# Output weights prepared inside the last unit of a layer, and the last attention begun behind the first half tile: a two-layer hybrid decoder step

## The reference

```python
u = rms_norm(x, norm_gain)
proj = einsum('btd,dc->btc', u, w_in)            # 1024 -> 3592 columns
h_m = sigmoid(mo) * mlstm(mq, mk, mv, gates)     # 4 heads, chunked memory
h_r = retention(rope(rq), rope(rk), rv)          # 4 heads, chunked memory
h_a = window_attention(aq, ak, av, sinks, bias)  # 8 heads, window 128
mix = concat(head_norm(h_m) * silu(mz), head_norm(h_r) * silu(rz), h_a * silu(az))
x = x + einsum('btc,cd->btd', mix, w_out)        # 1024 -> 1024
# after both layers
y = rms_norm(x, final_gain)
```

## Time and profile before

| | us |
|---|---|
| median of 3 runs | 2292.84 |
| lowest and highest run | 2283.0, 2296.8 |
| the profiled execution, whole | 2283.98 |
| its span, first to last instruction | 2282.2 |
| PE busy | 2166.6 (95%) |
| DVE busy | 1566.8 (69%) |
| ACT busy | 845.3 (37%) |
| mean granted TensorE clock | 0.977 |

### The profile page before, as it was taken

One profiled execution on the slowest core, in us unless ns is written; L12 is line 12 of the kernel. 1 busy time (PEld: TensorE's weight loads), 2 busy tenths in 40 slices (PEclk: granted clock), 3 DMA queues, 4 the chain that ended last, 5 costly groups with the idle time before them and its releaser, 6 DMA issues. The chain is left out here.

```text
span 2282.2 us, 37529 instructions
## 1 busy us (share of the span) xinstructions
PE 2166.6 (95%) x13387; PEld 1280.7 (56%) x13387; DVE 1566.8 (69%) x3881; ACT 845.3 (37%) x2250; POOL 317.1 (14%) x342
## 2 busy tenths in 40 slices
PE   4999999999999999899979999999999999999898
PEld 2456666666666666444444666666666666654343
DVE  6757767776777777566455677767777677787766
ACT  5733334344443335221145343443333343451000
POOL 1011111111111111120000111111111111111200
PEclk8999999999999999999989999999999999999989
DMA  9110000000000002965641000000000000146443
GB/s 286 61 27 21 20 23 35 20 20 20 20 21 20 20 20 93 193 189 144 168 122 48 27 26 20 20 20 20 21 20 20 25 32 20 44 126 161 129 106 97
DMA packets 137504, 143.61 MB, mean 63 GB/s; under 512 B 97207, under 2 KB 110328, under 8 KB 137276
## 3 DMA queue, kind: packets, MB, share of 16 engines
q1 hardware_dynamic: 118836, 108.60, 17.3%
q0 software_dynamic: 7424, 29.43, 3.9%
q10 hardware_dynamic: 11176, 4.68, 0.9%
HBM read 85.70 MB, written 42.31 MB: 56 GB/s over the span
## 5 line engine op out<-in xcount | busy, mean ns | idle before, releaser
L533 PE MATMUL J<-W,uT_mix 128*128 128x512 f16 (+2 forms) x6144 | 1214.0, 354 | 18.8 <-DVE W L526 8.4
L533 PEld LDWEIGHTS J<-W,uT_mix 128*128 128x128 f16 x6144 | 596.7, 98 | 562.5 <-DVE uT_mix L1552 16.6
L1261 ACT ACTIVATE PB<-J,out_scale 128x512 f32<-128x512 f32 (+2 forms) x256 | 154.6, 604 | 390.2 <-PE J L533 385.0
L1143 PE MATMUL J<-W,EM_qkR_mix 128*128 128x512 f16 x640 | 160.7, 391 | 0.0
L1143 PE MATMUL J<-W,uT_mix 128*128 128x512 f16 x560 | 135.6, 381 | 0.0
L1143 PEld LDWEIGHTS J<-W,EM_qkR_mix 128*128 128x128 f16 x640 | 64.5, 101 | 79.7 <-issue 9.6
L1552 DVE SCALAR_TENSOR_TENSOR uT_mix<-T,uT_mix 128x512 f16<-128x512 f32 x64 | 41.2, 684 | 88.4 <-ACT uT_mix L1185 85.6
L1589 DVE TENSOR_TENSOR ge<-ge,gr 128x512 f32<-128x512 f32 (+1 forms) x96 | 57.3, 597 | 63.2 <-ACT gr L1208 63.2
L1232 ACT ACTIVATE sc_xr<-sc_xr,small 128x128 f32<-128x128 f32 x256 | 98.6, 389 | 0.0
L533 PE MATMUL J<-W,gr 128*64 128x512 f16 (+2 forms) x384 | 83.1, 383 | 15.0 <-ACT qTA_part L1288 8.4
L912 PE MATMUL W<-PB,ST 128*128 128x64 f32 x512 | 96.6, 275 | 0.0
(11 more groups left out here) (438 smaller groups left out, 3469.7 us busy)
## 6 DMA issues: line engine op xcount, KB each, us to landing
mix_d<-ST SPq DMA_DIRECT2D x32, 512.5 KB, 2.8
W<-in_w_in POOLq DMA_DIRECT2D x8, 2048.0 KB, 15.1
x_mix<-in_x_prompt SPq DMA_DIRECT2D x16, 512.0 KB, 3.8
ST<-in_w_in POOLq DMA_DIRECT2D x4, 2048.0 KB, 12.4
W<-in_w_out SPq DMA_DIRECT2D x4, 2048.0 KB, 7.8
x_mix<-x SPq DMA_DIRECT2D x16, 512.0 KB, 3.8
PB<-in_x_prompt SPq DMA_DIRECT2D x6, 512.0 KB, 4.6
x<-PB SPq DMA_DIRECT2D x6, 512.0 KB, 6.8
```

Source lines behind the costliest of these rows:

```text
L533: mm = nc.tensor.matmul(out, stationary(k, a), moving[:, k, b, :], start=(k == 0 and n == 0), stop=(k == KT - 1 and n == 2))
L1143: mm = nc.tensor.matmul(J[n][0:rows, :], of_tile[:, s, k, :], w[:, cols], start=(k == 0 and i == 0), stop=(k == KT - 1 and i == 2))
L1261: return af(dst, src, ACT.Copy, scale=scale)
```

## The change

Four things change, in both layers alike.

1. ACT now sums six of the eight rows of W_out instead of four (`WO_SUMS` 4 to 6: 12 sums for 8), six sums before `em` and six where the eight stood. DVE takes the maxima of two rows instead of four.
2. The scale is made earlier: PE's `top_turn` and `top_spread` move ahead of the projection of aq and use bank T[0] instead of B[0]; DVE's join and `top_of_all` stand ahead of `m_result` and `w_out_scale` behind it.
3. All eight `hi` and `lo` rows are made inside the last unit (before: three there, five in the last attention). In exchange `mix_size`, `mix_hi` and `mix_lo` of that unit go behind all of them, and on ACT `mix_hi` goes behind the copy of az.
4. The last attention starts one half later: PE multiplies half 0 first, then does `keys` and `scores`; `turn` is behind half 3 instead of 2, `values` behind half 4 instead of 3, and all other steps move by one half as well. DVE does `r_result` at once, but `keys` and `scores` behind `residual` of half 0.

```diff
-        SUM_KS, WO_SUMS = 5, 4
+        SUM_KS, WO_SUMS = 5, 6
 def top_turn / top_of_all / top_spread:
-            bank = B[0] if j == W_OUT else B[3]
+            bank = T[0] if j == W_OUT else B[3]
 # PE, unit
                 m_out(n)
+                if not more:
+                    top_turn(pe, layer, W_OUT)
                 pe.wait_ge(E["o_read"], n)
                 r_turn(n)
+                if not more:
+                    top_spread(pe, layer, W_OUT)
                 project_block(n, "aq")
-                if not more:
-                    pe.wait_ge(E["rqk_ready"], n + 1)
-                    top_turn(pe, layer, W_OUT)
                 r_scores(n)
...
-                else:
-                    top_spread(pe, layer, W_OUT)
 # PE, last attention
-                pe.wait_ge(wo_scale_ready, layer + 1)
+                yield 0
+                pe.wait_ge(E["r_out_read"], NE)
                 keys(NE)
                 scores(NE, "full")
-                yield 2
+                yield 3
                 turn(NE)
-                yield 3
+                yield 4
                 values(NE, "full")
 # ACT, unit
                 gate_log(n, "m")
+                if not more:
+                    w_out_sums(act, layer, range(0, 6))
                 em(n)
...
                 if not more:
-                    act.wait_ge(w_out_loaded[0], 16 * (layer + 1))
-                    for k in range(2 * WO_SUMS):
-                        abs_sum(act, wo_tops[:, k:k + 1], w_out_sb[:, k // 2, k % 2 * 512:k % 2 * 512 + 512])
+                    w_out_sums(act, layer, range(6, 2 * WO_SUMS))
...
-                mix_hi(n)
-                evac(n, "aq")
-                gate_first(n, "r")
-                if not more:
+                if more:
+                    mix_hi(n)
+                    evac(n, "aq")
+                    gate_first(n, "r")
+                else:
+                    gate_first(n, "r")
                     act.wait_ge(E["m_out_psum"], n + 1)
                     w_out_hi(act, layer, range(0, 3))
+                    evac(n, "aq")
+                    w_out_hi(act, layer, range(3, KT))
                     act.wait_ge(E["gates_a"], n)
                     evac(n, "az")
+                    mix_hi(n)
 # ACT, last attention
                 queries(NE)
-                w_out_hi(act, layer, range(3, KT))
                 probs(NE)
-                yield 0
+                yield 1
...
 # DVE, unit
-                    w_out_max(dve, layer, slice(4, 6))
-                    w_out_max(dve, layer, slice(6, 8))
+                    w_out_max(dve, layer, slice(WO_SUMS, KT))
+                    dve.wait_ge(C["sum_ready"], LAYER_SUMS * (layer + 1))
+                    V.tensor_reduce(wo_max, wo_tops, AX.X, ALU.max).then_inc(wo_max_ready, 1)
+                    top_of_all(dve, layer, W_OUT)
                 m_result(n)
+                if not more:
+                    w_out_scale(dve, layer)
                 dve.wait_ge(E["mixmr_ready"], n)
                 m_gated(n)
+                if more:
+                    mix_size(n)
+                gate_inverse(n, "r")
                 if not more:
-                    dve.wait_ge(C["sum_ready"], LAYER_SUMS * (layer + 1))
-                    V.tensor_reduce(wo_max, wo_tops, AX.X, ALU.max).then_inc(wo_max_ready, 1)
-                mix_size(n)
-                if not more:
-                    top_of_all(dve, layer, W_OUT)
-                gate_inverse(n, "r")
+                    w_out_lo(dve, layer, range(0, 4))
                 r_weights(n)
                 if not more:
-                    w_out_scale(dve, layer)
-                if not more:
-                    w_out_lo(dve, layer, range(0, 3))
+                    w_out_lo(dve, layer, range(4, KT))
+                    mix_size(n)
                 mix_lo(n)
 # DVE, last attention
+                r_result(NE)
+                yield 0
                 keys(NE, "full")
-                r_result(NE)
-                w_out_lo(dve, layer, range(3, KT))
                 scores(NE, "full")
-                yield 0
+                yield 1
                 gate_cap(NE - 1, "a")
                 head_moments(NE, gr[:, 0:512])
-                yield 1
+                yield 2
                 head_scale(NE)
                 gate_inverse(NE - 1, "a")
-                yield 2
+                yield 3
                 part_probs(NE, "full")
-                yield 3
+                yield 4
                 values(NE)
-                yield 4
+                yield 5
                 mix_size(NE)
-                yield 5
+                yield 6
                 mix_lo(NE)
```

More of the change, by code:

```diff
@@ L287, in build @@
         junk = sb("junk", [P, 2, 512], BF16)
-        wo_small = sb("wo_small", [P, 17])
+        wo_small = sb("wo_small", [P, 19])
         small_n = sb("small_n", [TS, 18])
@@ L490, in top_spread @@
         def top_spread(pe, layer, j):
-            bank = B[0] if j == W_OUT else B[2]
+            bank = T[0] if j == W_OUT else B[2]
             pe.wait_ge(C["top_ready"], top_count(layer, j))
@@ L586, in build @@
         w_out_loaded = [sem(f"w_out_loaded{i}") for i in range(2)]
-        c_wo = Chain("dve_w_out", 7)
+        c_wo = Chain("dve_w_out", 6)
         wo_max_ready = sem("wo_max_ready")
         wo_scale_ready, wo_hi_ready, wo_lo_ready = map(sem, ["wo_scale", "wo_hi", "wo_lo"])
-        wo_tops, wo_max, wo_m, wo_e, wo_s, wo_inv = (wo_small[:, a:b] for a, b in ((0, 12), *((12 + i, 13 + i)
+        wo_tops, wo_max, wo_m, wo_e, wo_s, wo_inv = (wo_small[:, a:b] for a, b in ((0, 14), *((14 + i, 15 + i)
                                                                                                for i in range(5))))
@@ L1239, in attention_act, with w_out_sums @@
             return gate_log, gate_first, gate_exp, queries, head_rstd, probs, mix_hi
+        def w_out_sums(act, layer, halves):
+            for i in halves:
+                act.wait_ge(w_out_loaded[i // KT], 16 * (layer + 1))
+                abs_sum(act, wo_tops[:, i:i + 1], w_out_sb[:, i // 2, i % 2 * 512:i % 2 * 512 + 512])
         def w_out_hi(act, layer, ks):
@@ L1684, in w_out_max @@
             dve.wait_ge(w_out_loaded[1], 16 * (layer + 1))
-            c_wo.step(nc.vector.tensor_reduce(wo_tops[:, ks.start + 4:ks.stop + 4], w_out_sb[:, ks, :], AX.X, ALU.max, apply_absolute_value=True))
+            c_wo.step(nc.vector.tensor_reduce(wo_tops[:, ks.start + WO_SUMS:ks.stop + WO_SUMS], w_out_sb[:, ks, :], AX.X, ALU.max, apply_absolute_value=True))
         def w_out_scale(dve, layer):
@@ L1689, in w_out_scale @@
             dve.wait_ge(C["top_spread"], top_count(layer, W_OUT))
-            st(V.tensor_copy(wo_m, B[0][:, 256:257]))
+            st(V.tensor_copy(wo_m, T[0][:, 256:257]))
             st(V.tensor_scalar(wo_m, wo_m, TINY, None, ALU.max))
```

4 lines of the change are left out of this document (2 added, 2 removed).

## The result

Twelve runs of the changed kernel, beside twelve of the kernel before: 2295.35 us median (2289.61 to 2303.39) against 2285.27 (2281.54 to 2296.8), a ratio of 1.0042, 95% interval 1.0026 to 1.0058. The change costs 6 to 13 us, about 10. The forecast named 2295.5, but from a start of 2292.84 (three runs) that twelve runs put at 2285.27: the place is right and the step, +2.7, is a quarter of what was measured.

What follows compares the result with a forecast made beforehand. PE, busy 95% of the span, was taken as the bound, its stall before scores costing 6.0 us a layer. Layer 0's -2.3 and layer 1's +5.0 gave +2.7 on 2292.84: 2295.5 us, range 2281 to 2307.

Steps and rivals of the forecast that it cites:

- The last unit: Last unit before the output stage: r_out ends at 910.5 instead of 910.30, and half 0 starts without a wait.
- `lo(7)`, the mix, the residual rows: End of last unit: lo(7) ends 912.5, mix ready 917.0, SP loads tile 0's residual rows at 917.5, landing 922.3.
- The new wait: Last attention, behind half 0: PE waits 2.5 us before keys and 4.6 before scores, 7.1 in place of 4.61.
- Layer 0: Layer 0's output stage: tile 3 starts 2.3 us earlier than 962.76, bounds a gain of 6 and a loss of 3.
- The rival that SP's lateness comes through: Output stage: turn holds SP 7.8 us and tile 3's mix lands late; +13 us in all, 2306; chance 0.22.
- Layer 1, the term that was mis-sized: Layer 1's output stage: DVE is the limit, values wait 4.5 us for part_probs; 5.0 us lost, bounds 2 and 7.
- the old stall: PE's 4.61 us wait for r_result before scores in the kernel before; with 1.4 us of slow clock, 6.0 us a layer.
- The start: Median of the kernel before that the forecast added its step to: 2292.84 us.
- The first rival: Last attention: the half tile covers everything and both stalls go with their clocks, at most 12 us, 2281; chance 0.17.

Runs made afterwards that it cites:

- e1: Changed kernel with DVE copying the last attention's keys ahead of half 0's residual instead of behind it: 2295.57 us, ratio 1.0042.
- e2: Changed kernel with SP loading tile 0's residual rows ahead of the store of the mix in the last unit: 2292.22 us, ratio 1.0030.
- e3: Changed kernel with mix_size, mix_hi and mix_lo of the last unit ahead of all split rows of W_out: 2289.88 us, ratio 1.0027.
- e4: Changed kernel with DVE's stretch of the last attention ahead of the final norm at odd halves, layer 1 only: 2287.5 us, ratio 1.0012.
- g1: Changed kernel: mix size and split before W_out's rows, r_weights behind two, PE awaits aq's copy before half 0, attention tail before layer 1's final norm: 2277.05 us, 0.995.
- f1: Changed kernel without part 4, so the last attention begins at once and its steps stand at their old halves: 2295.42 us, ratio 1.0039.
- f2: Changed kernel with the edits of e2 and e4 together: 2284.25 us, ratio 0.9995.
- f3: f2 with r_result and the copies of the queries and keys woven into the last unit: 2295.08 us, ratio 1.0054.
- f4: f3 with turn, part_probs, values and the last chunk's mix one half earlier: 2292.51 us, ratio 1.0038.

## Why the prediction was right, and where not

- **The last unit.** From the second piece of `m_out` to the end of `r_out` it takes 14.36 us instead of 14.10 (896.19 to 910.29 before, 897.37 to 911.73 now): +0.26, forecast +0.2. Half 0 waits for nothing. Right. The places below are shifted by the 1.2 us that this profile is late before the stage.
- **`lo(7)`, the mix, the residual rows.** Forecast 912.5, 917.5 for SP's residual load, 922.3 for its landing; measured 914.1, 919.1 and 923.7, less the 1.2: 912.9, 917.9, 922.5. Right. The 512 KB took 4.6 us from issue to use (4.8 in the earlier trace rows). The estimate of 3.2 us from the Trainium skill, page DMA: Bandwidth & Descriptors, section Anatomy of one DMA, is not what this trace shows.
- **The new wait.** Forecast 2.5 us before `keys` and 4.6 before `scores`, half 1 16.4 us behind `r_out`; measured 2.77, 3.81 and 16.98 (16.65 in layer 1). Right, and e1, e2 and e3 show that the late rows and DVE's order make the second wait and the late mix the first.
- **Layer 0.** Forecast a gain of 2.3 at tile 3, measured 0.2 (52.47 to 52.29), within the bounds. `turn` held SP somewhat longer than forecast: the residual load came at 945.93, 944.7 less the 1.2, for a forecast 943.3, and the transpose at 952.52, 951.3 less the 1.2, for 949. It was 8.3 us in flight instead of 14.8, and PE then waited 3.2 us more for the token scales. Both causes that the prediction named agree with the table above: the small transfers ahead of tile 0's store (5.3 us in flight now, 8.3 before) and POOL's load beside the transpose. The rival that SP's lateness comes through put its mark at 8 us; with 8.3 the transfer lay at that mark, and the layer neither gained the 2.3 nor lost the 4 to 5 us. The Trainium skill, page Trainium Kernel Development and Optimization, section Quick Reference, has SP's and POOL's transfers share the same 16 engines; the trace agrees, with the flights of both doubling together.
- **Layer 1, the term that was mis-sized.** Forecast 5.0 us lost by half 6 (bounds 2 and 7), measured 10.66, outside the bounds. The wait for `part_probs` was right (4.5 forecast, 4.61 measured). What the sum left out is the clock behind both waits: half 1 takes 6.23 instead of 5.18 us, `values` 6.89 instead of the 3.6 that I had carried over, half 5 6.16 instead of 5.18. That is 1.05 + 3.3 + 1.0 = 5.3 us of the 5.7 missed. I had priced the half clock behind the old stall at 1.4 us in the first paragraph, and `scores` at it, and then costed `values` behind a new wait of 4.5 us at the full clock. The row that should have warned is the earlier trace rows: a wait of 4.61 us had cost it. e4, without that wait, returns 7.4 us of layer 1, and some 0.3% of the whole.
- **The start.** 2292.84, the median of three runs, was 7.6 us above that of twelve. The missing 7.6 of the start and the missing 7.4 of the loss cancel; that the number was met is luck, and only the sign, the two waits and the one for `part_probs` are to its credit.
- **The first rival** said that a mix ready sooner would take out both stalls with their clocks, at most 12 us, 2281. As a forecast of this change it was wrong. g1, which stores the mix at 904.73, comes near that case, with e4's order besides: 0.5%, 11.4 us below the kernel before, with an interval of 5 to 18.

## What to carry to other kernels

A wait that halves the granted clock costs the slow stretch behind it as well; price every new wait of some microseconds twice, with the usual duration of the instructions behind it and with the one they have at 1.2 GHz, and take both as bounds. Here the second was what happened behind the new waits of 2.77, 3.81 and 4.61 us. When work is pulled forward on an engine, look at what has been pushed behind it and who issues transfers on it: here a stored mix, three links away from PE, became the release of two waits. A step put "behind the first half tile" inherits all that this half's DVE work waits for.

## What the runs showed of the hardware

- **The clock and the length of a wait.** Behind waits of 2.77 and 3.81 us and of 4.61 us the clock is at 1.2 GHz for the next 5 to 9 us; behind 1.91 us and behind four waits of 0.3 to 0.7 us in g1 it stays at 2.4. `scores` take 3.78 us at the one and 2.00 at the other. The length alone does not decide. In f1 `values` of layer 1 waited only 1.03 us, ran 1.8 us at full speed and then at 1.2 GHz, 5.26 us in all instead of 3.6. In layer 1, ahead of half 25, PE waits 3.0 us for the same DVE operation in all fourteen profiles: in eleven the clock stays at 2.4 GHz behind it, in f2, f3 and f4 it falls to 1.2. e3's wait of 2.25 us ahead of `r_out` is followed by 7 us at 1.2 GHz, while ahead of half 30 of layer 0 the kernel before waits 3.01 us and runs on at full speed. What sets it these runs leave open. The row of that half 30:

```profile
1135.32 0.39 PE L1143 MATMUL J<-vaug_kw_wo,EM_qkR_mix 128*128 128x512 f16 x1 [3.01 <-DMA tok_raw<-mix_d]
```

- **DVE beside POOL.** The first split row takes 1.75 us in the changed kernel, 1.28 before, with the same operands; POOL runs two products in that time:

```profile
902.66 0.73 POOL L2088 TENSOR_TENSOR ge<-ge,PB 128x256 f32<-128x256 f32 x1 [7.66 <-DVE ge L1601]
903.47 1.59 POOL L2089 TENSOR_TENSOR ge<-ge,head_g 128x256 f32<-128x256 f32 x1
```

  The second of these takes 1.59 us, and 0.72 in the kernel before, where no split row runs beside it. The second split row takes 1.75 us as well. POOL's second product ends 0.6 us behind the end of the first row, a little less than its own 0.72, so the two may take turns rather than share; no run here parts them.
- **Scatter.** The kernel before ran between 2269.33 and 2303.04 us in 34 runs of one comparison, g1 between 2270.28 and 2285.13 in 12. The mean granted clock goes with it: 0.981 at 2269.33, 0.972 at 2303.04. That g1 spreads less may be its fewer long waits, but twelve runs against 34 do not show it.
